# Down projections of a two-layer trunk with each product over 128 rows taken as two over 64 rows

## What is computed

```python
D_MODEL, SEQ, D_FF = 1024, 256, 2816
def swiglu(x, w_gate, w_up, w_down):
    return (jax.nn.silu(x @ w_gate) * (x @ w_up)) @ w_down

for layer in range(2):
    h = h + 0.5 * swiglu(rms_norm(h, ln_ffn1[layer]), ...)
    u = rms_norm(h, ln_mix[layer])
    h = h + (diff_attention(u, ...) if layer == 0 else swa_sink_attention(u, ..., k_band, v_band))
    h = h + 0.5 * swiglu(rms_norm(h, ln_ffn2[layer]), ...)
    if layer == 0:
        k_band, v_band = shared_kv(h, ...)
return rms_norm(h, final_norm)
```

## Time and profile before

| what | value |
|---|---|
| median of 3 runs | 925.05 us (924.87 to 925.78) |
| span of the profiled execution | 923.1 us |
| TensorE busy | 913.7 us, 99% of the span |
| TensorE weight loads busy | 749.6 us, 81% |
| VectorE busy | 568.9 us, 62% |
| ScalarE busy | 471.4 us, 51% |
| GpSimd busy | 94.8 us, 10% |

### The profile page before, as it was taken

How to read it: one execution, slowest core, us unless ns; L and a number is a source line. 1 busy time by engine, 2 the same in 40 slices (tenths; PEclk the granted TensorE clock), 3 DMA queues, 4 the chain that set the end, 5 groups by cost and what they waited for, 6 DMA issues and landing times.

```text
span 923.1 us, 11582 instructions
## 1 busy us (share of the span) xinstructions
PE 913.7 (99%) x4235; PEld 749.6 (81%) x4235; DVE 568.9 (62%) x616; ACT 471.4 (51%) x638; POOL 94.8 (10%) x172
## 2 busy tenths in 40 slices
PE   9999999999999999999999999999999999999997
PEld 7888888878878888888888888888876778888885
DVE  5656663674587756665468566654578775656542
ACT  6544543465686645444445545433468664444431
POOL 1100006534311100000002000000030010000000
PEclk9999999999999999999999999999999999999999
DMA  9798677656522788876557788874672288888621
GB/s 307 247 300 250 228 254 229 214 193 230 184 92 92 221 264 269 248 256 225 184 177 242 235 250 249 305 244 167 198 274 93 92 278 257 264 248 287 223 83 45
DMA packets 166877, 200.75 MB, mean 217 GB/s; under 512 B 14840, under 2 KB 136768, under 8 KB 166832
## 3 DMA queue, kind: packets, MB, share of 16 engines
q1 hardware_dynamic: 165872, 199.27, 66.5%
q0 software_dynamic: 512, 0.36, 0.5%
q10 hardware_dynamic: 448, 0.53, 0.2%
HBM read 183.34 MB, written 16.78 MB: 217 GB/s over the span
## 4 chain that ended last, share of the span: by engine, by line
PE 95%; DVE 2%; issue 1%; ACT 1%; DMA 1%; SPq 0%; POOL 0%; POOLq 0%; ACTq 0%
PE bank L513 59%; PE bank L552 19%; PE bank L558 9%; PE bank L574 2%; PE bank L744 1%; PE bank L617 1%; DVE w_lo L1742 1%; PE bank L797 1%; PE bank L719 1%; PE bank L775 1%; DMA x<-in_x 1%; PE bank L737 1%; DVE xT_lo L1774 0%; ACT w_hi L1359 0%; DVE x L1789 0%
## 5 line engine op out<-in xcount | busy, mean ns | idle before, releaser
L1742 DVE TENSOR_TENSOR w_lo<-raw,w_hi 128x2048 fp32r<-128x2048 f32 x153 | 349.5, 2292 | 193.8 <-ACT w_hi L1359 193.5
L1359 ACT ACTIVATE w_hi<-raw 128x2048 fp32r<-128x2048 f32 x154 | 294.7, 1917 | 194.5 <-PE bank L558 100.0
L513 PE MATMUL bank<-w_hi,xT_hi 128*128 128x512 f32 x816 | 319.4, 391 | 0.9 <-DVE w_lo L1742 0.9
L513 PE MATMUL bank<-w_lo,xT_hi 128*128 128x512 f32 x816 | 317.6, 389 | 0.0
L513 PE MATMUL bank<-w_hi,xT_lo 128*128 128x512 f32 x816 | 307.9, 389 | 0.0
L513 PEld LDWEIGHTS bank<-w_hi,xT_hi 128*128 128x128 f32 x816 | 153.2, 188 | 34.1 <-DVE w_lo L1742 2.3
L513 PEld LDWEIGHTS bank<-w_hi,xT_lo 128*128 128x128 f32 x816 | 153.2, 188 | 32.2
L513 PEld LDWEIGHTS bank<-w_lo,xT_hi 128*128 128x128 f32 x816 | 153.2, 188 | 31.4
L552 PE MATMUL bank<-w_hi,hT_hi 128*128 128x512 f32 x348 | 135.6, 390 | 0.0
L552 PE MATMUL bank<-w_lo,hT_hi 128*128 128x512 f32 x348 | 135.4, 389 | 0.0
L558 PE MATMUL bank<-w_hi,hT_lo 128*128 128x512 f32 x348 | 107.2, 389 | 0.0
(11 more groups left out here) (182 smaller groups left out, 601.5 us busy)
## 6 DMA issues: line engine op xcount, KB each, us to landing
raw<-in_ffn_w_down SPq DMA_DIRECT2D x88, 512.0 KB, 5.1
raw<-in_ffn_w_gate SPq DMA_DIRECT2D x86, 512.0 KB, 5.9
raw<-in_ffn_w_up SPq DMA_DIRECT2D x86, 512.0 KB, 7.2
raw<-in_a_w_qkv SPq DMA_DIRECT2D x24, 512.0 KB, 5.4
h_bounce<-silu SPq DMA_DIRECT2D x40, 256.0 KB, 6.5
xn<-h_bounce SPq DMA_DIRECT2D x160, 64.0 KB, 3.4
xn<-x_bounce SPq DMA_DIRECT2D x64, 64.0 KB, 2.0
raw<-in_a_w_o SPq DMA_DIRECT2D x8, 512.0 KB, 5.2
```

What stands on the lines that cost most here:

```text
L513: mm = nc.tensor.matmul(bank[b][:, :], xs[:, kt, own(pos)], ws[:, slot(u), cols], start=(kt == 0 and i == 0), stop=(kt == KT - 1 and i == 2))
L1359: nc.scalar.activation(w_parts(u)[0], raw[:, slot(u), :], ACT.Copy).then_inc(s_hi, 1)
L1742: nc.vector.tensor_tensor(lo, raw[:, slot(u), :], hi.bitcast(F32), ALU.subtract).then_inc(s_lo, 1)
```

## The change

Only TensorE's program changes. For units 0 to 6 of both pos, for units 7 to 10 of pos 0 and unit 7 of pos 1, each product over 128 rows becomes two over 64 rows: rows 0 to 63 go into one bank and rows 64 to 127 into the other bank of the same pos, side by side. A pass of a unit (`half_rows_pass`) therefore does half of the work for each bank; a second pass, with the halves swapped, does the other half ("crossing"). Before the second pass TensorE waits on a new semaphore, `s_crossed`, for the last product of the first pass. The order is now by unit: first pass for pos 0, first pass for pos 1, second pass for pos 0, second pass for pos 1. Units 7 to 10 of pos 0 go in one first and one second pass, with unit 7 of pos 1 between and after. Units 8 to 10 of pos 1 stay as they were.

```diff
+            def half_rows_pass(u, kt0, pos, lhs_hi, lhs_lo, swap, fresh=False, closing=False):
+                for k in range(2):
+                    kt = kt0 + k
+                    for i, (lhs, ws) in enumerate(((lhs_hi, w_hi), (lhs_hi, w_lo), (lhs_lo, w_hi))):
+                        for j in range(2):
+                            rows = slice(HD * (swap ^ j), HD * (swap ^ j) + HD)
+                            cols = slice(D * k + BANK * j, D * k + BANK * (j + 1))
+                            mm = nc.tensor.matmul(bank[acc(pos, j)][:, :], lhs[rows, kt, own(pos)],
+                                                  ws[rows, slot(u), cols], start=(fresh and k == 0 and i == 0),
+                                                  stop=(closing and k == 1 and i == 2))
+                return mm
...
+            def crossed(mm):
+                mm.then_inc(s_crossed, 1)
+                crossings[0] += 1
+                return crossings[0]
...
-                pe.wait_ge(s_hT_lo[0], block_no(f, H_BLOCKS - 1))
-                down((0, 1, 2), 0)
-                pe.wait_ge(s_hT_lo[1], block_no(f, H_BLOCKS - 2))
-                down((0, 1, 2), 1)
-                down((3, 4, 5, 6), 0)
-                down((3, 4, 5, 6), 1)
-                down((7, 8, 9, 10), 0)
-                down((7,), 1)
+                swap = 0
+                for i in range(7):
+                    done = []
+                    for pos in range(NPOS):
+                        if i == 0:
+                            for j in range(2):
+                                take(acc(pos, j))
+                        done.append(crossed(half_rows((i,), pos, swap, i == 0)))
+                    swap ^= 1
+                    for pos in range(NPOS):
+                        pe.wait_ge(s_crossed, done[pos])
+                        mm = half_rows((i,), pos, swap)
+                    mm.then_inc(s_used, 1)
+                late = (7, 8, 9, 10)
+                done = [crossed(half_rows(late, 0, swap)), crossed(half_rows((7,), 1, swap))]
+                swap ^= 1
+                pe.wait_ge(s_crossed, done[0])
+                fill(half_rows(late, 0, swap, closing=True), ("down", f))
...
+                pe.wait_ge(s_crossed, done[1])
+                half_rows((7,), 1, swap).then_inc(s_used, 1)
```

More of the change, by code:

```diff
@@ L247, in trunk @@
         s_used = sem("s_used")
+        s_crossed = sem("s_crossed")
         s_filled = sem("s_filled")
@@ L568, in rows_pass @@
                         note((*key, pos, j), acc(pos, j))
+            crossings = [0]
+            def half_rows_pass(u, kt0, pos, lhs_hi, lhs_lo, swap, fresh=False, closing=False):
[13 more added lines that the diff above has]
+                return crossings[0]
             def transposes(srcs, b, key, turn=None):
@@ L682, in down, with half_rows @@
                         rows_pass(u0 + GU_UNITS + i, 2 * i, FT, pos, hT_hi, hT_lo, ("down", f))
-                pe.wait_ge(s_hT_lo[0], block_no(f, H_BLOCKS - 1))
-                down((0, 1, 2), 0)
-                pe.wait_ge(s_hT_lo[1], block_no(f, H_BLOCKS - 2))
-                down((0, 1, 2), 1)
-                down((3, 4, 5, 6), 0)
-                down((3, 4, 5, 6), 1)
-                down((7, 8, 9, 10), 0)
-                down((7,), 1)
+                def half_rows(ts, pos, swap, fresh=False, closing=False):
+                    for i in ts:
+                        if pos == 0:
+                            unit_ready(u0 + GU_UNITS + i)
+                        if i % 2 == 0 and i < DN_UNITS - 1:
+                            pe.wait_ge(s_hT_lo[pos], block_no(f, i // 2))
+                        if i == DN_UNITS - 1:
+                            pe.wait_ge(s_last_lo[pos], f + 1)
+                        mm = half_rows_pass(u0 + GU_UNITS + i, 2 * i, pos, hT_hi, hT_lo, swap,
+                                            fresh and i == ts[0], closing and i == ts[-1])
+                    return mm
+                swap = 0
[16 more added lines that the diff above has]
+                fill(half_rows(late, 0, swap, closing=True), ("down", f))
+                for j in range(2):
+                    note(("down", f, 0, j), acc(0, j))
+                pe.wait_ge(s_crossed, done[1])
+                half_rows((7,), 1, swap).then_inc(s_used, 1)
                 if next_name:
```

## The result

The changed kernel takes 955.1 us (median of 4 runs, 952.27 to 956.29); the kernel before, run beside it, 925.04 us (924.87 to 925.78). The ratio is 1.032, with a 95% interval of 1.0303 to 1.0338: 30 us slower. The prediction was 950 us, range 934 to 964.

A forecast was written before the change was run, and what follows sets the result against it. TensorE's products times their distance bound the kernel, waits adding in full. Terms 0 + 1.6 + 15.0 + 2.1 + 0.4 + 2.7 + 3.0 = 24.8 us on 923.1 gave 947.9, with 1.95 for the median about 950; range 934 to 964.

The forecast's parts named there:

- What bounds the kernel: TensorE, busy 99% of the span: time is number of products times their distance, and any wait is added in full.
- Part 1, the halves: Down projections: 912 products become 912 pairs, each still 0.2267 us because the gap stays with float32r; 0 us.
- the gap closing: Rival for the pairs in the down projections: a pair takes 0.216 us, -9.8 us, total 940; chance 0.22.
- the gap paid twice: Rival for the pairs: each weight load costs a gap, 0.240 us per pair, +12.2 us, total 962; chance 0.14.
- no side by side: Rival for the pairs: float32r halves run one after the other, 0.427 us or more, +183 us, total 1133; chance 0.09.
- Part 2, entering and leaving: Each down projection enters and leaves 64-row products once, 0.2 us each time; 8 x 0.2 = +1.6 us.
- Part 3, bank 2: Start of each down projection: TensorE waits for VectorE's L1835 to free bank 2; 4 x 3.75 = +15.0 us.
- Part 4, unit 10: TensorE waits for down unit 10's split, 0.43 us plus about 0.1 for restarting; 4 x 0.53 = +2.1 us.
- Part 5, the end of pos 0: Pos 0 completes 1.36 us nearer the phase's end; +1.36 us behind f = 0 and f = 2, together +2.7 us.
- The clock: TensorE's granted clock falls in some of the four bank waits: between 0 and 12.8 us, taken as +3.0 us.
- The rival with the clock up in all four: No clock fall in the four waits, gap unchanged, total 947; within the forecast's case, together 0.48.
- the faster rival: Pair at 0.216 us and bank 2's wait gone: -3.4 us, 921.7 us; needs waits under about 0.4 us; chance 0.04.

The follow-up runs named there:

- experiment 6: Changed kernel with bank 2 freed before unit 3's split, units 0 and 1 in pos 0's first passes, units 7 to 10 as before: 927.85 us.
- experiment 7: Kernel before, with whole row products of the down projections reading only the upper 16 bits of both operands as bfloat16: 923.9 us.
- experiment 8: Kernel of experiment 6, with the halves reading only the upper 16 bits of every operand as bfloat16: 925.64 us.
- Experiment 1: Changed kernel's order on TensorE kept, but each product taken whole over 128 rows instead of in halves: 954.51 us.
- experiment 2: Changed kernel with silu and VectorE's product that frees bank 2 moved ahead of the split of down unit 3: 935.75 us.
- experiment 3: Changed kernel with pos 0's first passes covering units 0 and 1, twelve pairs ahead of the bank wait: 944.51 us.
- experiment 5: Changed kernel with bank 2 freed ahead of unit 3's split and units 7 to 10 as in the kernel before: 932.05 us.
- experiment 4: Changed kernel with units 7 to 10 in whole products and order as in the kernel before: 949.81 us.

## Why the prediction was right, and where it was off

**What bounds the kernel.** Right. TensorE's stream sets the time, and each wait put into it appeared in full: 28.7 us of terms explain 29.1. The median of the changed kernel lies another 1 us above its profiled execution, whose granted clock was 0.990; the two slowest of the four runs had 0.986 and 0.987.

**Part 1, the halves.** The value was right: 0.227 us for a pair, by the timelines after and in experiment 6. Of its rivals, the gap closing (940), the gap paid twice (962) and no side by side (1133) are all excluded by the same rows. The reason given was right only in part, so the value owes something to luck. I argued that the gap is there with float32r at any number of rows, because the earlier trace rows lack it and differ in type. The number of rows does not matter, as experiment 6 shows, and the trace of the kernel before could have said so: its plain float32 products over all 128 rows lack the gap too, one of 128 columns each (0.60 - 0.273) / 3 = 0.109 us, where two cycles a column make 0.107:

```profile
699.97 0.60 PE L574 MATMUL bank<-ident,xn 128*128 128x128 f32 x4
```

But float32r is not what brings it; experiments 7 and 8 show it with bfloat16, at 0.225 to 0.2267. The bfloat16 products of the earlier trace rows, which lie packed, show it as well: of the eight steps between two of them with 512 columns that the trace has, seven are 0.226 or 0.227 us and one is 0.215. What sets plain float32 apart is a third thing, which the prediction named and did not weigh, that it streams at two cycles a column; whether this is what hides the gap was not tested.

The Trainium skill's rule, in "TensorE: Matmul & The Clock Gate", section Part 3, that a weight load overlaps a running product only in another row group, would have given the halves an advantage. The trace does not agree: experiment 6 has the same load of 0.19 us beside each pair and no gain. The 4 ns that the Trainium skill gives there for each further tile does not show in the period either: it is 0.2267 with one tile and with two.

**Part 2, entering and leaving.** Right in size: 0.09 us of gap and 0.11 us of late weights at each change of rows, and experiment 6 confirms both without the other waits. Experiment 8 ties the 0.11 to the weights. "TensorEngine Tiling (Array Packing)", section Key Properties, of the Trainium skill says that changing the tiling mode drains TensorE. The trace agrees in so far as the first product behind each change starts 0.32 us after the last one in place of 0.227.

**Part 3, bank 2.** Right, and the heart of the case: 3.75 predicted, 3.69 measured, four times, on the line and the releaser that were named. Experiment 1 shows that it belongs to the order, experiment 2 that VectorE's queue makes it, experiment 3 that each 1.36 us of work ahead of it shortens it by as much.

**Part 4, unit 10.** Right: the step from 176.81 to 177.53 is 0.49 us over a pair, and 0.11 for the late second pair, 2.4 us in all against 2.1.

**Part 5, the end of pos 0.** Half right. Behind f = 0 the wait rose from 0.48 to 1.39, behind f = 2 from nothing to 0.95, both less than the 1.36 I took: I had counted the whole move and left out two things. TensorE leaves the halves on the way, so it comes 0.2 us later. And VectorE's chain got shorter. In f = 2 its first two splits behind pos 0's result take 4.49 us from start to end in place of 4.71 (after, then before):

```profile
684.80 4.49 DVE L1791 TENSOR_TENSOR w_lo<-raw,w_hi 128x2048 fp32r<-128x2048 f32 x2 [2.28 <-ACT w_hi L1408]
662.32 4.71 DVE L1742 TENSOR_TENSOR w_lo<-raw,w_hi 128x2048 fp32r<-128x2048 f32 x2 [2.28 <-ACT w_hi L1359]
```

So the chain of the earlier trace rows, which I took to have no slack, stood still for 0.2 us between these splits. With both, 1.36 us becomes the 0.95 measured. Behind f = 0 the two splits took 0.58 us less than before, and TensorE came 0.3 us sooner, because the transpose of the norm gains cost it 0.07 us in place of 0.41: 1.36 - 0.2 - 0.58 + 0.34 = 0.92, against 0.91. Behind f = 1 I predicted nothing, and there stands a new wait of 0.24 us for `hT_lo`, which grew to 0.8 in experiment 5.

**The clock.** This is the term that was mis-sized, 3.0 for 7.4 us, and it is nearly the whole difference between 947.9 and 952.2 of span. I expected falls in some of the four and part of the low time inside the waits. The falls came in all four, and late: in three of four the low stretch lies behind the wait, on working time. The upper bound that I had, 12.8 us, held. A better estimate was to be had from the same rows: the fall of the earlier trace rows came 2.3 us or more after TensorE had stopped, and the low clock lasted, so each of four waits of 3.75 us could bring one, and most of a low time that begins late in a wait falls on the work behind it.

**Range and rivals.** The 2 us between forecast median and span were right (954.05 - 952.2 = 1.85). The rival with the clock up in all four (947) is excluded by the windows; the faster rival needed the bank wait gone and the gap closed. Experiment 6 took the wait away, but the gap stayed, so it ended at 927.85. By its own sum that rival would have borne a wait of up to 3.4 / 4 = 0.85 us in each phase, not 0.4.

## What to carry to other kernels

When an order is rearranged, look at every resource that the moved work needs first (a bank, a slot, a split) and at when its producer, in its own fixed order, is done; the move costs the difference each time it occurs, and a wait in TensorE's stream can cost more than itself (here 3.5 us each, and another 1.6 to 2.6 us of lost clock). Moving the producer's release ahead of one long instruction got back 19 of 30 us here, more than any single edit on TensorE. Splitting a product that already fills all 128 rows into halves side by side gives the same streaming time and costs the changes of mode.

## What the runs showed of the hardware

- Two 64-row float32r products of 512 columns run side by side at full rate: a pair every 0.227 us, like one of 128 rows. The kernel before had only plain float32 halves.
- The granted clock fell in all four phases with waits of 3.5 to 3.8 us (here and in experiments 1 and 4), in two of four with 2.15 to 2.21 us (experiment 3), and in none with 0.8 to 1.0 us (experiments 2 and 5). The low stretches of the down projections lasted 3.41 or 6.83 us. The four runs of the changed kernel spread over 4 us, with a mean granted clock from 0.991 (952.27 us) to 0.986 (956.29 us); the four of the kernel before over 0.9 us.
- The gap of 0.013 us behind a float32r product of 512 columns stays with 64 rows, and with bfloat16 and half the weight load time it is 0.0117 us in three phases and 0.0133 in the fourth (experiments 7 and 8). With 256 columns of float32r it is the same 0.013. Plain float32, at two cycles a column, has 0.002 to 0.003 us with 128 rows and with 64. What the gap is stays open.
- Loading 128 x 128 weights took 0.10 us in bfloat16 and 0.19 us in float32r. Both fit inside a product's 0.213 us of streaming, and experiment 7, which has the shorter one, is 1 us in 925 shorter.
